# Seven pieces of operand splitting and PSUM reading moved in a two-block transformer kernel, and the second half's sum and norm put first at each mixer's exit

## The reference

```python
def hybrid_mixer(x, cos, sin, w_in, ...):          # x: 256 tokens x 1024
    proj = x @ w_in
    (dq, dk, dv, dz, da, dbeta, glu, c_q, c_kv, k_r, gate_logits) = split(proj)
    y_dn = deltanet_branch(...)      # causal conv of q,k,v; chunked gated delta rule (triangular solve)
    y_cv = conv_branch(glu, ...)     # 31-tap depthwise conv, layer norm, silu, @ w_pw2
    y_mla = mla_branch(...)          # low-rank q and kv, rope, causal block attention, @ w_o
    gates = sigmoid(gate_logits + b_gate)
    merged = gates[0] * y_dn + gates[1] * y_cv + gates[2] * y_mla
    return merged @ w_out
h = layer_norm(ALPHA * h + mix)
h = layer_norm(ALPHA * h + 0.5 * swiglu_2(h))
```

## Time and profile before

| | |
|---|---|
| time, 3 runs | 2564.73 us median (2560.03 to 2567.55) |
| the profiled execution | 2573.43 us, span 2571.7 us |
| PE | 2433.6 us busy, 95% of the span |
| PEld | 2073.6 us, 81% |
| DVE | 1644.2 us, 64% |
| ACT | 1083.3 us, 42% |
| POOL | 317.4 us, 12% |
| mean granted TensorE clock | 0.976 |

### The profile page before, as it was taken

One profiled execution on the slowest core, in us unless ns is written; L12 is line 12 of the kernel. 1 busy time (PEld: TensorE's weight loads), 2 busy tenths in 40 slices (PEclk: granted clock), 3 DMA queues, 4 the chain that ended last, 5 costly groups with the idle time before them and its releaser, 6 DMA issues.

```text
span 2571.7 us, 35417 instructions
## 1 busy us (share of the span) xinstructions
PE 2433.6 (95%) x13082; PEld 2073.6 (81%) x13082; DVE 1644.2 (64%) x1780; ACT 1083.3 (42%) x1228; POOL 317.4 (12%) x419
## 2 busy tenths in 40 slices
PE   4999989999999899999998999999999999998998
PEld 3777868878879788888898888788788898887886
DVE  5888457778876655644667666555545667757455
ACT  3434454354453534443344344444344443344443
POOL 3110201101102000100007300000100026100000
PEclk8999989999999999999999999999999999999999
DMA  8896329859955566456342434555555331534554
GB/s 292 303 330 241 131 88 330 300 169 351 325 194 180 185 224 215 155 190 218 109 126 75 134 115 148 172 187 198 165 190 201 120 91 50 166 123 140 191 184 147
DMA packets 336354, 479.23 MB, mean 186 GB/s; under 512 B 19868, under 2 KB 278267, under 8 KB 336235
## 3 DMA queue, kind: packets, MB, share of 16 engines
q1 hardware_dynamic: 313434, 398.43, 47.1%
q0 software_dynamic: 22800, 79.23, 8.3%
HBM read 476.55 MB, written 1.05 MB: 186 GB/s over the span
## 4 chain that ended last, share of the span: by engine, by line
issue 53%; PE 28%; POOLq 6%; DVE 5%; DMA 3%; POOL 2%; DVEq 2%; ACT 1%; SPq 0%; ACTq 0%
PE ps L925 9%; PE ps L927 9%; PE ps L926 9%; POOLq L896 3%; POOLq L900 2%; DMA probs<-in_w_ada_dram 2%; DVE mix_mem L2257 2%; DVE w_lo L2145 2%; DVEq L2273 1%; POOL n_rstd L735 1%; DMA out_sb<-in_w_ada_dram 1%; PE ps L991 1%; DMA raw<-in_ffn_wu_dram 1%; ACT w_hi L1694 0%; POOL rstd L729 0%
## 5 line engine op out<-in xcount | busy, mean ns | idle before, releaser
L2145 DVE TENSOR_TENSOR w_lo<-raw,w_hi 128x2048 fp32r<-128x2048 f32 (+1 forms) x373 | 827.0, 2220 | 452.7 <-ACT w_hi L1694 447.5
L1694 ACT ACTIVATE w_hi<-raw 128x2048 fp32r<-128x2048 f32 (+1 forms) x370 | 689.3, 1866 | 396.5 <-PE ps L927 347.8
L925 PE MATMUL ps<-w_hi,x_hi 128*128 128x512 f32 x1440 | 578.9, 402 | 22.0 <-DVE x_lo L2164 9.3
L927 PE MATMUL ps<-w_hi,x_lo 128*128 128x512 f32 x1440 | 566.9, 394 | 0.0
L926 PE MATMUL ps<-w_lo,x_hi 128*128 128x512 f32 x1440 | 566.7, 394 | 0.0
L925 PE MATMUL ps<-x_hi,w_hi 128*128 128x256 f32 (+1 forms) x1120 | 331.3, 296 | 10.9 <-DVE w_lo L2145 10.4
L925 PEld LDWEIGHTS ps<-w_hi,x_hi 128*128 128x128 f32 x1440 | 274.7, 191 | 80.7 <-issue 9.6
L926 PE MATMUL ps<-x_lo,w_hi 128*128 128x256 f32 (+1 forms) x1120 | 323.9, 289 | 0.0
L927 PE MATMUL ps<-x_hi,w_lo 128*128 128x256 f32 (+1 forms) x1120 | 323.9, 289 | 0.0
L927 PEld LDWEIGHTS ps<-w_hi,x_lo 128*128 128x128 f32 x1440 | 273.8, 190 | 59.6
L926 PEld LDWEIGHTS ps<-w_lo,x_hi 128*128 128x128 f32 x1440 | 274.5, 191 | 54.9 <-issue 0.5
(11 more groups left out here) (416 smaller groups left out, 3006.3 us busy)
## 6 DMA issues: line engine op xcount, KB each, us to landing
raw<-in_w_in_dram SPq DMA_DIRECT2D x96, 512.0 KB, 4.5
raw<-in_ffn_w_gate_dram SPq DMA_DIRECT2D x90, 512.0 KB, 4.0
raw<-in_ffn_w_up_dram SPq DMA_DIRECT2D x90, 512.0 KB, 4.9
raw<-in_ffn_wg_dram SPq DMA_DIRECT2D x88, 512.0 KB, 4.6
raw<-in_ffn_wu_dram SPq DMA_DIRECT2D x88, 512.0 KB, 5.8
raw<-in_ffn_wd_dram SPq DMA_DIRECT2D x80, 512.0 KB, 5.3
raw<-in_ffn_w_down_dram SPq DMA_DIRECT2D x80, 512.0 KB, 3.9
spare<-in_w_ada_dram POOLq DMA_DIRECT2D x46, 512.0 KB, 6.1
```

The source lines that it names most:

```text
L925: pe.matmul(dst, wh, vh, start=start, stop=False, skip_group_check=True)
L927: return pe.matmul(dst, wl, vh, start=False, stop=stop_, skip_group_check=True)
L1694: return f(w_hi[s][:, cols], raw[s][:, cols], ACT.Copy)
L2145: return v.tensor_tensor(w_lo[s][:, cols], raw[s][:, cols], w_hi[s][:, cols].bitcast(F32), ALU.subtract)
```

## The change

Seven pieces move, and one wait is added.

1. ScalarE, groups 0 to 5: the next chunk is rounded before the group's Silu, no longer after it.
2. ScalarE: group 11's bank is read after the decay exponentials; VectorE's product with it moves behind its work on them.
3. VectorE: the rests of chunks 16 and 17 come before the first levels; 18 before and 19 after the first copy for the levels; 20 two levels later. ScalarE rounds chunk 20 in two halves, one level apart.
4. VectorE: the rest of chunk 21 comes after `low` has been scaled.
5. Attention: `w_pw2`'s first chunk becomes the fill of items 6 and 7, into banks 7 and 3; group 28's reading moves from item 5 to item 6; the rest of chunk 33 comes after the attention. TensorE waits for a second `branch_free` ahead of chunk 35's products.
6. ScalarE and VectorE: chunk 39 is split before the last quarter of `merged` is rounded and its rest taken.
7. VectorE at the exit: sum and norm of the second half before the rest of chunk 42.

```diff
 # TensorE
+                def branch_part(j, first, bank, ms=None, waits=True):
+                    cols_chunk(bank, y_hi, y_lo, kt=4, n=512, first=first, ms=ms,
+                               waits=(lambda i: pe.wait_ge(y_lo_ready, call_y(l, 2 * j) + i // 2 + 1)) if waits else None)
...
                         cols_chunk(3 if g % 2 == 0 else 7, x_hi, x_lo, ms=(m,))
+                    elif it == 6:
+                        pe.wait_ge(evac, evac0 + 28)
+                        branch_part(1, 0, 7, (0, 1))
+                    else:
+                        pe.wait_ge(evac, evac0 + 29)
+                        branch_part(1, 0, 2, (2, 3), False)
                 attention(l * 8 + 8, 1, score, v_mla, first, fill)
-                pe.wait_ge(evac, evac0 + 29)
-                branch(1, 0, 4)
-                branch(2, 4, 0)
+                branch_part(1, 0, 4, waits=False)
+                branch(2, 4, 0, lambda: pe.wait_ge(branch_free, 2 * l + 2))
 # ScalarE
                     last.then_inc(evac, 1)
+                    ahead(n0 + pos(g) + 4)
                     act_qkv(g)
...
-                for g in range(8, 12):
+                def glu_out(g):
...
+                for g in range(8, 11):
+                    glu_out(g)
                 act.wait_ge(dec_in, l + 1)
...
                     .then_inc(dec_exp, 1)
+                glu_out(11)
...
                     if s == 1:
-                        ahead(n0 + 21)
+                        ahead(n0 + 20)
+                        first_half()
+                    elif s == 2:
+                        second_half()
...
                 def between(it):
-                    if it in (0, 1, 3, 5):
-                        gate_out((25, 26, None, 27, None, 28)[it])
-                    elif it == 6:
+                    if it in (0, 1, 3, 6):
+                        gate_out((25, 26, None, 27, None, None, 28)[it])
+                    elif it == 5:
+                        ahead(n0 + 34)
+                    elif it == 7:
                         ahead(n0 + 35)
...
-                    if i == 2:
-                        ahead(e + 3)
+                    if i >= 2:
+                        ahead(e + i + 1)
                     y_round(0, 6 * l + (9 + i), merged, i)
 # VectorE
-                evacuated(11)
-                v.tensor_tensor(glu[:, 2:4, :], glu[:, 2:4, :], sig[:], ALU.mult).then_inc(glu_ready, 1)
                 dve.wait_ge(dec_exp, l + 1)
...
+                evacuated(11)
+                v.tensor_tensor(glu[:, 2:4, :], glu[:, 2:4, :], sig[:], ALU.mult).then_inc(glu_ready, 1)
                 ahead(n0 + 16)
...
                 v.tensor_tensor(amat[:], amat[:], tmat[:], ALU.mult).then_inc(a_ready, 1)
+                ahead(n0 + 18)
...
                 level(1).then_inc(b_ready, 1)
-                ahead(n0 + 18)
...
-                ahead(n0 + 20)
+                ahead(n0 + 19)
...
                 d_out(l * HALVES + 1)
+                ahead(n0 + 20)
...
-                    if s == 1:
+                    if s == 3:
                         ahead(n0 + 21)
...
-                ahead(n0 + 22)
...
                 last.then_inc(hd_scaled, 1)
+                ahead(n0 + 22)
...
-                    elif it in (1, 2, 4, 5):
-                        ahead(n0 + (None, 31, 32, None, 33, 34)[it])
+                    elif it in (1, 2, 4):
+                        ahead(n0 + (None, 31, 32, None, 33)[it])
...
+                    src = ps[:, (7, 3, 4, 5)[m // 2], T * (m % 2):T * (m % 2) + T]
...
+                last.then_inc(branch_free, 1)
...
+                    if i == 4:
+                        ahead(n0 + 40)
...
-                ahead(n0 + 43)
                 chunk_done(n0 + 40)
                 centred_x(n, 1)
                 scaled_x(n, 1)
+                ahead(n0 + 43)
```

More of the change, by code:

```diff
@@ L1569, in branch @@
                             second()
-                        cols_chunk(bank + 2 * c, y_hi, y_lo, kt=4, n=512, first=first,
-                                   waits=(lambda i: pe.wait_ge(y_lo_ready, call_y(l, 2 * j) + i // 2 + 1))
-                                   if c == 0 else None)
+                        branch_part(j, first, bank + 2 * c, waits=c == 0)
                 branch(0, 0, 4, lambda: pe.wait_ge(mla_sb, l * 3 + 1))
                 proj(21)
-                pe.wait_ge(branch_free, l + 1)
+                pe.wait_ge(branch_free, 2 * l + 1)
                 for h in range(HEADS):
@@ L1975, in gate_out @@
                     if br == 1 and j == 0:
-                        act.wait_ge(branch_free, l + 1)
+                        act.wait_ge(branch_free, 2 * l + 1)
                     src = ps[:, 3 if g % 2 == 0 else 7, :] if br == 2 else bank(g)
@@ L2939, in mix_b @@
                 for m in range(KT):
-                    v.scalar_tensor_tensor(out=gate[:, m, :], in0=ps[:, 4 + m // 2, T * (m % 2):T * (m % 2) + T], scalar=cols1[:, CB_PW2 + m:CB_PW2 + m + 1],
-                                           in1=gate[:, m, :], op0=ALU.add, op1=ALU.mult)
+                    src = ps[:, (7, 3, 4, 5)[m // 2], T * (m % 2):T * (m % 2) + T]
+                    last = v.scalar_tensor_tensor(out=gate[:, m, :], in0=src, scalar=cols1[:, CB_PW2 + m:CB_PW2 + m + 1],
+                                                  in1=gate[:, m, :], op0=ALU.add, op1=ALU.mult)
+                last.then_inc(branch_free, 1)
                 dve.drain()
```

## The result

| | before | after |
|---|---|---|
| median, us | 2566.11 (2560.03 to 2567.55, 4 runs) | 2529.18 (2527.03 to 2531.91, 4 runs) |
| profiled execution, us | 2573.43 (span 2571.7) | 2527.62 (span 2525.9) |
| mean granted TensorE clock | 0.976 | 0.981 |

The four runs of before hold the three shown earlier. The ratio is 0.9862 (95% 0.9846 to 0.9878); in a later set of runs it was 0.9871 (0.9851 to 0.9892). The forecast was 2529.

A forecast was written before the change was run, and what follows sets the result against it. TensorE was taken as the bound, busy 338.22 of 364.00 us in the first mixer. Waits of 16.15 and 15.25 us made 31.4, plus 4.6 for clock, 36: median 2564.73 becomes 2529, range 2513 to 2548.

The forecast's parts named there:

- groups 0 to 5: Mixer entry: rounding ahead of the Silu ends TensorE's waits for chunk rests and the kr copy; 3.2 us, first mixer.
- decay, chunk 16, levels: First mixer: exponentials in time 2.1 us, chunk 16's rest and first level copy 3.2, chunk 20's halved rounding 0.8.
- `low`: Scaling of low ahead of chunk 21's rest: 1.6 us wait goes, part moves to line 1135; gain 1.2, first mixer.
- attention: Attention items 6 and 7: TensorE's waits of 2.2 and 1.6 us for weights go; gain 3.8 in the first mixer.
- `w_out`: Before w_out: chunk 39's rest comes earlier, its wait of 2.40 us becomes 1.4; gain 1.0 in the first mixer.
- exit: Mixer exit: norm wait of 4.9 us shrinks by 2.1, new wait of about 1.2 on chunk 42; gain 0.85.
- clock: Seven half-clock stretches behind waits that should go or shrink, worth 0 to 11.9 us; taken as 4.6.
- the first rival: Both mixers: the clock comes back whole, 31.4 + 11.9 = 43 us gained, 2521; chance 0.18.
- wait at chunk 35: After attention: sign against the forecast; with a time above 2548 it would speak for the bound by VectorE.
- load that holds ScalarE in the groups: Groups 0 to 5: a late load stalls a moved rounding and all behind it; 4.4 us each, 53 lost in twelve.
- the tail: Rival: from 1566 on VectorE becomes the bound, 5.65 us given back twice, gain 20, 2545; chance 0.20.
- the slower case: Rival: roundings moved ahead wait for loads and hold ScalarE in all twelve groups, 53 us lost against 31, 2587; chance 0.04.

The follow-up runs named there:

- the filler: Kernel of rest 22 later plus eleven unread products in TensorE's wait at the end of each mixer; 2513.08 us, ratio 0.9805.
- rest 22 later: Changed kernel with chunk 22's rest moved behind the delta net's eight diagonals on VectorE; 2513.76 us, ratio 0.9799.
- early load: Changed kernel with dn_w_o's loads issued ahead of SyncE's wait for the third product and the uq and ukv loads; 2519.65 us, ratio 0.9831.

## Why the prediction came out, and where it was wrong

The time, 2529, was right; the terms, for both mixers, against the idle time that undoing each piece brings back:

| term | predicted | measured |
|---|---|---|
| groups 0 to 5 (piece 1) | 6.4 | 7.7 |
| decay, chunk 16, levels (2, 3) | 11.3 | 11.2 |
| `low` (4) | 2.4 | -3.1 |
| attention (5) | 7.6 | 5.4 |
| `w_out` (6) | 2.0 | 4.6 |
| exit (7) | 1.7 | 1.7 |
| sum of waits | 31.4 | 27.1 |
| clock | 4.6 | 11.4 |
| both | 36.0 | 38.5 |

The measured column is what undoing a piece adds to TensorE's idle time; its last three rows are the whole change, so the six terms above them add up to 27.5 and not to 27.1.

- Entry, decay, chunk 16, levels: right by their steps, but for one reading: the decay exponents were not there long before, ScalarE now waits 4.1 us for VectorE to make them, and is in time all the same. The two waits of 0.3 to 0.4 on line 1503 are there at 0.33 each.
- `low` was the step that failed. The prediction saw the move to line 1135 and its cause, and took 0.4 for the new wait, with 2.6 as the bound; it was 4.36 and 3.26. Counted from line 1135's first matmuls behind the third product, TensorE came to line 1135 after 19.05 us before and would have come after 14.31 now: 1.58 by the wait that went, but 3.2 more nearly all of it because its sums and group 19's projection ran at full clock (2.51 and 8.19 us became 1.71 and 5.99). The diagonals came 0.8 later (18.6 after, 17.8 before). 0.4 + 3.2 + 0.8 is the 4.4. The last term is this one mixer's: in the other thirteen with the same order the wait is 2.9 to 3.4 us, and the diagonals come after 17.1 to 17.7 us. The working had set the new arrival by the old durations, and those held the very clock loss that the change was to take away. And the term is not merely smaller: the piece as placed loses time, 3.5 us where it acts.
- Attention: both waits are gone, 3.8 a mixer as forecast, and bank 3's products were in time. Undoing the piece brings back less, 5.4: 2.2 on line 1155 and only 1.0 on line 1166, while line 1135's wait is 2.89 there in the first mixer.
- `w_out`: chunk 39's wait shrank to 0.59, not 1.4, and chunk 42's rest comes earlier with it (1.5 to 0.9 on its wait).
- Exit: 2.86 and 0.90, against 2.8 and 1.2.
- Clock: 11.4, so what the first rival had (11.9), not 4.6. It was not whole, though: 74.2 us of the two stretches were at 1.2 GHz before, where the prediction counted 23.8 as open, and 54.0 still are. Nor are they in the same places: the times at 1.2 GHz behind the waits of the attention and of `w_out` (from 1558.7 and 1596.2) are gone, and new ones begin at 1400.7 and 1496.3, where before had none.
- The sum: the right total came of two errors, -4.3 on the waits and +6.8 on the clock, and that they nearly cancel is luck. The profiled execution came 9 below the 2537 forecast for it, 7.2 of them ahead of the mixers.
- The rivals: no wait at chunk 35 and no load that holds ScalarE in the groups, so neither the tail nor the slower case. But one load already late became the costliest wait of the changed kernel.

## What to carry to other kernels

A wait on the bounding engine is worth its length plus what the granted clock loses behind it, here 1.6 us became 4.7 where nothing else held up the next step; so work out when that engine arrives at the next thing from full-clock durations, not from the old trace's. Before moving work earlier, look at what the next needed item stands behind in its engine's order: if it is queued behind a step that waits for a load, the gain ends there, and letting the short step that someone waits for go ahead of it (one moved line, some 15 us) is worth more than the move. And undo each piece of a change that succeeded: of these seven pieces, one cost time and one brought none that could be measured.

## What the runs showed of the hardware

- The clock's loss behind a wait is not in proportion to it: a wait of 1.58 us was followed by 3.2 us of loss in one order (chunk 19's projection 8.37 instead of 6.00), and by about 1.5 (7.48) behind the same wait in the kernel with piece 4 alone undone. Between executions of one kernel the stretches at 1.2 GHz lie at other places; TensorE's busy time in the mixers was 670.8 and 673.1 in two of them.
- All of that difference, and that between the kernels, is the clock, within 3 us: busy time less half of the time at 1.2 GHz is 643.7 to 646.6 us for the two stretches in each of the thirteen profiles without the filler, while the time at 1.2 GHz goes from 30.0 to 74.2. With piece 5 undone, waits of 2.2, 0.5 and 0.6 us in the attention go with 6.8 us of it, in both mixers; in the kernel before, 3.8 us of waits at the same place go with 3.4.
- VectorE's write of the eight diagonals (128x1024) took 1.68 us in the changed kernel's first mixer, and the rest of chunk 22 (128x2048) ahead of it 2.50; in its second mixer they took 1.21 and 2.46, and in both mixers of its second profile 1.22 and 2.29. The kernel before had 1.21 behind 2.69, and 1.61 behind 2.29. With rest 22 later or with the early load the diagonals took 1.22 to 1.23 in every mixer. Why the longer times come and go was not tried.
- `dn_w_o`'s first chunk (1 MB, two issues of 512 KB), issued behind SyncE's wait for the third product and behind 2.2 MB of `uq` and `ukv`, made ScalarE wait 4.33 and 4.91 us in the changed kernel, 4.25 and 4.27 with rest 22 later. Issued ahead of both it made nobody wait, and the two larger loads were still in time. Which of the two held it longer no run separates.
